# A decoder layer on one core: the value products of the first head pair placed before the next scores, and another order at the end of the merged stage

## The reference

```python
h = rmsnorm(x, attn_norm[l]) * (1.0 + scale_a) + shift_a
proj = h @ w_in[l]
y_mla = mla_mix(...)   # 8 heads, causal: softmax(qn kn + qp kp) @ v, then rmsnorm
y_gdn = gdn_mix(...)   # 4 heads, gated delta rule over chunks, then rmsnorm * silu(gate)
x = x + gate_a * (jnp.concatenate([y_mla, y_gdn], axis=-1) @ w_out[l])
h = rmsnorm(x, moe_norm[l]) * (1.0 + scale_m) + shift_m
x = x + gate_m * hierarchical_moe(h, ...)   # top group, top 2 of its 8 experts
return rmsnorm(x, final_norm)
```

## Time and profile before

| | us |
|---|---|
| median of 3 runs (2413.59 to 2421.41) | 2417.65 |
| the profiled execution, its own time | 2419.23 |
| its span, first to last instruction | 2417.5 |
| the merged stage in it | about 693 to 1476 |
| the output stage in it | 1476 to 1776 |

### The profile page before, as it was taken

How to read it: one execution, slowest core, us unless ns; L and a number is a source line. 1 busy time by engine, 2 the same in 40 slices (tenths; PEclk the granted TensorE clock), 3 DMA queues, 4 the chain that set the end, 5 groups by cost and what they waited for, 6 DMA issues and landing times. The chain is left out here.

```text
span 2417.5 us, 35480 instructions
## 1 busy us (share of the span) xinstructions
PE 2182.2 (90%) x11479; PEld 1243.3 (51%) x11480; DVE 987.8 (41%) x2202; ACT 872.1 (36%) x2123; POOL 631.6 (26%) x1108
## 2 busy tenths in 40 slices
PE   5999999999977998999999996999939999999990
PEld 2545555545444666666666673555534444444440
DVE  2334343433255575665566652234351222222223
ACT  2264363462655654555555561111111111111113
POOL 1000000000024542634542501233322222222224
PEclk9999999999988999999999998999969999999995
DMA  9212121120352344343343329333305788999777
GB/s 345 83 62 77 44 77 62 42 75 33 107 190 77 113 154 143 92 130 117 112 140 108 99 73 324 147 121 124 122 18 169 222 253 268 301 328 291 223 220 302
DMA packets 221896, 361.77 MB, mean 150 GB/s; under 512 B 45579, under 2 KB 143526, under 8 KB 218294
## 3 DMA queue, kind: packets, MB, share of 16 engines
q1 hardware_dynamic: 207926, 309.57, 37.6%
q0 software_dynamic: 13824, 50.34, 8.5%
HBM read 259.93 MB, written 99.93 MB: 149 GB/s over the span
## 5 line engine op out<-in xcount | busy, mean ns | idle before, releaser
L704 PE MATMUL pV<-keys_values_then_all,w_in_sb 128*128 128x512 f32 x768 | 341.3, 598 | 4.7 <-DMA w_in_sb<-in_w_in_dram 4.7
L2190 PE MATMUL hidden_ps<-w,keys_values_then_all 128*128 x752 | 331.5, 594 | 0.4 <-SPq L2062 0.4
L1252 ACT ACTIVATE probs<-scores,neg_max 128x512 f32<-128x512 f32 (+3 forms) x320 | 195.0, 621 | 227.6 <-DVE neg_max L1363 152.9
L704 PEld LDWEIGHTS pV<-keys_values_then_all,w_in_sb 128*128 128x128 f32 x768 | 145.1, 192 | 178.0 <-issue 177.3
L2190 PEld LDWEIGHTS hidden_ps<-w,keys_values_then_all 128*128 128x128 f32 x752 | 143.4, 191 | 180.6 <-issue 180.5
L1828 PE MATMUL out_ps<-keys_values_then_all 128*128 128x512 f32 x512 | 226.3, 601 | 2.5 <-ACT keys_values_then_all L1677 2.5
L2120 ACT ACTIVATE keys_values_then_all<-hidden_ps 128x256 f32<-128x256 f32 x47 | 18.0, 383 | 454.7 <-PE hidden_ps L2190 454.7
L2200 PE MATMUL expert_ps<-w_sb,keys_values_then_all 128*128 x368 | 169.8, 604 | 0.0
L1828 PEld LDWEIGHTS out_ps<-keys_values_then_all 128*128 128x128 f32 x512 | 97.2, 192 | 121.8 <-issue 116.2
L1169 POOL TENSOR_TENSOR keys_values_then_all<-keys_values_then_all 32x31 f32<-32x31 f32 (+15 forms) x248 | 120.5, 486 | 117.9 <-DMA keys_values_then_all<-a_d 98.7
L1508 PE MATMUL scores<-keys_values_then_all,queries 64*128 64x512 f32 (+3 forms) x640 | 148.0, 584 | 0.0
(11 more groups left out here) (371 smaller groups left out, 3196.6 us busy)
## 6 DMA issues: line engine op xcount, KB each, us to landing
w<-in_w_dram SPq DMA_DIRECT2D x64, 1024.0 KB, 10.4
w_sb<-in_w_dram SPq DMA_DIRECT2D x32, 1024.0 KB, 13.7
keys_values_then_all<-in_x_dram SPq DMA_DIRECT2D x32, 512.0 KB, 5.3
w_mod_rows<-in_w_mod_dram SPq DMA_DIRECT2D x16, 1024.0 KB, 4.9
keys_values_then_all<-in_w_mod_dram SPq DMA_DIRECT2D x4, 2048.0 KB, 15.0
qkv_d<-l_out SPq DMA_DIRECT2D x32, 256.0 KB, 2.3
keys_values_then_all<-y_d SPq DMA_DIRECT2D x16, 512.0 KB, 4.6
x_d<-keys_values_then_all SPq DMA_DIRECT2D x16, 512.0 KB, 2.9
```

The costliest lines, as they stand in the source:

```text
L704: last = pe.matmul(pV[n % 2][:], win[:, k, QKV0 + c * P:QKV0 + (c + 1) * P], hT[:, s % 2, k, :], start=(k == 0), stop=(k == ND - 1))
L1252: act.activation(prob[:, e, 0:w].rearrange("p t k -> p (t k)"), pS[e][:, 0:w * P], ACT.Exp, scale=-1.0, bias=nmin[:, i % 2, h, b:b + 1], a ...
L2190: last = pe.matmul(pH[par][:], xT[par][:, k], m.w13[:, ds(slot, 1), k].rearrange("p s n -> p (s n)"), start=(k == 0), stop=(k == ND - 1))
```

## The change

In `mix_order` the value products of a quad are two atoms instead of one. V(j, 0) comes behind T2 T3 and ahead of the first O and of S(j+1), V(j, 1) stays where both were; each costs half. The chain steps of the cost 0.325 n that stood between S(j+1) and V(j, 0) thereby come ahead of S(j+1). The steps held back (O2, G) go in behind V(j, 1), as before. In the last atoms BX(15) changes places with AS(14), and O2(15) comes behind the last O instead of ahead of it. SP loads the gate of chunk n+1 at TR(n) instead of at O2(n), with the same wait. In `output`, PE no longer waits at the start for the routing weights and for `pick`, but where it first uses them.

```diff
@@ -735,18 +735,19 @@
         if i > 1 and first and TILE[i - 1] < 4:
             atoms.append((0.0, [("AS", i - 2, 0)]))
         turns = [(0.13 * (TILE[i - 1] // 4 + 1), [("O", i - 1, hp)]) for hp in (2 * o, 2 * o + 1)] * (i > 0 and o < AH // 4)
+        atoms.append((0.325 * n, [("V", j, 0)]))
         atoms += turns[:1]
         if ahead:
             atoms.append((0.8 * ahead, [("S", j + 1)] + [("X", j + 1, e) for e in range(4)]))
         if i and last and TILE[i] >= 4:
             atoms.append((0.0, [("AS", i - 1, 0)]))
-        atoms.append((0.65 * n, [("V", j, 0), ("V", j, 1)]))
+        atoms.append((0.325 * n, [("V", j, 1)]))
         atoms += turns[1:]
         if i and o == AH // 4 - 1:
             atoms.append((0.0, [("A", i - 1, 0)]))
         if last:
             atoms.append((0.0, [("B", i, 0)]))
-    atoms.append((0.0, [("AS", NT - 2, 0), ("BX", NT - 1, 0), ("B2", NT - 1, 0)]))
+    atoms.append((0.0, [("BX", NT - 1, 0), ("AS", NT - 2, 0), ("B2", NT - 1, 0)]))
     for o in range(AH // 2):
         atoms.append((0.44, [("O", NT - 1, o)]))
     atoms.append((0.0, [("A", NT - 1, 0), ("AS", NT - 1, 0)]))
@@ -796,12 +797,12 @@
         while atoms and owed >= atoms[0][0]:
             owed -= atoms[0][0]
             order += atoms[0][1]
-            if atoms.pop(0)[1][0][0] == "V":
+            if atoms.pop(0)[1][0][::2] == ("V", 1):
                 order += held
                 held = []
-    order += held
-    for _, kinds in atoms:
+    for _, kinds in atoms[:-1]:
         order += kinds
+    order += held + atoms[-1][1]
     return quads, order
 
 
@@ -1089,6 +1090,9 @@
                     sp.dma_start(m.inv_d[n * (P - QK):(n + 1) * (P - QK), :], both_T).then_inc(inv_stored, 16)
                 elif kind == "L":
                     load_inverses(n)
+                elif kind == "TR" and n + 1 < NT:
+                    wait(yg_stored, 16 * n)
+                    load_gate(n + 1)
                 elif kind == "KS" and n + 2 < NT:
                     wait(ks_ready, n + 1)
                     load_kq(n + 2)
@@ -1101,9 +1105,6 @@
                         for r in range(8):
                             sp.dma_start(m.mod_d[0:1, r * 512:(r + 1) * 512], mod_sum[32 * (r % 4):32 * (r % 4) + 1, r // 4]).then_inc(mod_stored, 16)
                 elif kind == "O2":
-                    wait(yg_stored, 16 * n)
-                    if n + 1 < NT:
-                        load_gate(n + 1)
                     wait(yg_ready, n + 1)
                     sp.dma_start(m.y_d[n * P:(n + 1) * P, AH * DV:], gates[:, n % 2].rearrange("p h d -> p (h d)")).then_inc(yg_stored, 16)
                 elif kind == "V" and step[2] == 1 and n in last_j:
@@ -1809,8 +1810,6 @@
             start_counts(pe, sems[4::5])
             wait = waiter(pe)
             pe.wait_ge(m.wo_loaded, 16 * 2)
-            pe.wait_ge(m.wr_loaded, 16 * 6)
-            pe.wait_ge(pick_made, 3)
 
             def body(n, par, ty, mm, rt, lg):
                 if n in RANK_AT:
@@ -1847,6 +1846,8 @@
                     if n >= RANK_AT[0]:
                         pe.wait_ge(rank_read, sum(at <= n for at in RANK_AT))
                     pe.wait_ge(halves_copied, n - 1)
+                    if n == 2:
+                        pe.wait_ge(pick_made, 3)
                     wait(logit_read, n - 2)
                     pe.matmul(pL, halves_T[:], pick[:], start=True, stop=True).then_inc(logit_ready, 1)
                 if rt:
@@ -1854,6 +1855,8 @@
                     wait(h2T_dve, n)
                     if n > 1:
                         pe.wait_ge(halves_copied, n - 1)
+                    else:
+                        pe.wait_ge(m.wr_loaded, 16 * 6)
                     for k in range(ND):
                         at = 64 * (k % 2)
                         last = pe.matmul(pLT[at:at + NR, :], wr[:, k], h2T[:, k], start=(k < 2), stop=(k >= ND - 2))
```

## The result

| | before | after |
|---|---|---|
| median of the runs, us | 2416.38 (2413.59 to 2421.41) | 2440.93 (2435.03 to 2451.04) |
| profiled execution: time, span, us | 2419.23, 2417.5 | 2435.03, 2433.3 |
| TensorE busy, us | 2182.2 | 2202.0 |

The changed kernel is slower: ratio 1.01 with a 95 % interval of 1.0077 to 1.0123, +24.5 us between the medians. The forecast was 2434, slower. The two profiled executions differ by only 15.8 us, because that of after happens to be the fastest of its four and that of before lies 2.9 above its median. What follows compares the two profiles; the first experiment, whose profile lies on its median, supplies the rest.

What follows compares the result with a forecast made beforehand. The prediction saw TensorE, busy 2182.2 of 2417.5 us, waiting on a loop between scores through DVE and ACT. Terms +29.6 - 9 + 3 - 5.5 - 1.9 = +16.2 on 2419.2 gave 2435.4, stated as 2434; range 2396 to 2454.

Steps and rivals of the forecast that it cites:

- S wait: Merged stage: TensorE's waits ahead of the scores for copies of turned probabilities fall from 37.8 us to 2.7.
- V wait: Merged stage: V(j, 0) waits for the copies of heads 0 and 1, 53.8 us, 58 places over 0.1.
- The T wait: Merged stage: the transposes T wait 10.9 us more for their exponentials.
- No instruction is added: Merged stage: splitting the pair only moves 80 half value products of up to 0.95 us and adds no instruction.
- The other waits: Merged stage: TensorE's remaining waits, 28.5 us, partly shrink behind longer ones; from 0 to -28.5, taken as -9.
- The clock: Merged stage: more waits over 1.7 us, about 10 instead of 5, lower TensorE's clock; -6 to +15, taken as +3.
- The rival in which the clock gives everything back: Merged stage: waits cut too short to lower the clock bring 30 us back, 2401 us; chance 0.02.
- The last steps: Merged stage's end: BX(15) ahead of AS(14) and the earlier gate load end the stage sooner, -5.5 us.
- TensorE's start: Output stage: without the wait for POOL's `pick` TensorE starts at once, -1.9 us; later waits 0.
- the first (V waits for nothing): Merged stage: V(j, 0) fills the gap because ACT's copies come earlier; 2386 us, half of it 2400; chance 0.22.
- The second (waits only change their names): Merged stage: new waits at V and T replace chain waits one for one; 2411 us, or 2425; chance 0.22.
- The third (ACT's loop becomes the bound): Merged stage: with V(j, 0) inside ACT's loop other waits don't shrink; +37, 2455 us; chance 0.06.

Runs made afterwards that it cites:

- the first experiment: Kernel before with only the split: V(j, 0) its own atom ahead of the first O and S(j+1), end and loads as before; 2441.73 us, ratio 1.0119.
- third kernel: Changed kernel with V(j, 0) reading a constant tile, without its wait for copies; 2451.32 us, ratio 1.0156, later parts longer because other experts are chosen.
- ninth kernel: Kernel before with O placed between V(j, 0) and V(j, 1) in the 30 quads that have an O behind both; 2413.38 us, ratio 0.9988.
- second kernel: Changed kernel with the V pair together again as before; end order, gate load and output start stay changed; 2412.4 us, ratio 0.9998.
- seventh: Changed kernel with the V pair together again and the last tile's A and AS in another buffer; 2414.08 us, ratio 0.9988.
- fifth kernel: Changed kernel with head 1's copy moved from ACT to DVE, so each copies two turned heads; 2432.35 us, ratio 1.006.

## Why the prediction was right, and where its numbers were not

**Direction and place were right.** The S wait was to go and a V wait to come in its place: -37.6 and +43.8 measured, -35.1 (37.8 down to 2.7) and +53.8 in the sum. The third kernel shows the mechanism by taking the copies away, the first that the split alone does it.

**The V wait was mis-sized**, 53.8 for 43.8. I had placed V(j,0) by the planner's costs, but kept the ends of the copies where they were before; chain work that moved ahead of S may have left ACT freer between exponentials and copies. That this is the reason was not shown.

**The T wait** was put at +10.9. As a wait it came out at -2.4; but the T steps are 11.1 longer. Of the 224 T steps of full width, which take 0.44 us at the least, 25 took over 0.6 in before and 51 in after, and none more than 0.66, near the pace of the exponentials (0.67 each by the prediction's 1097.58 to 1100.25). I had written that L1516's wait would rise from 4.6 to 10 to 20, and it fell to 2.5. That T(j,0) to T(j,2), 6.6 us longer in all, follow the exponentials in step is argued from that pace; no run took it apart. The other 4.5 us are T(j,3)'s. At full width it takes 0.53 us ahead of V(j,0) also in most quads of the third kernel, where V hardly waits, so that a good part of it is the price of the place and not a wait for exponentials. That the whole came out at 11.1, next to the 10.9 of the sum, is in part luck.

**"No instruction is added" was the step that failed.** The moved products were costed at nothing, and cost 12.2 us; the ninth kernel shows it as a fixed price for each pair. The trace of before already had a sign of it: the same 16 products took 0.924 as V(j,0), which V(j,1) follows, and 0.974 as V(j,1), which something else follows. That missing term, 12.2, and the waits at S and V, which were over-sized by 12.5 (18.7 in the sum, 6.2 measured), nearly cancel. That 2434 came out near is luck to this extent.

**The other waits** shrank by 8.6, for 9 forecast. That was a third of a bound from 0 to -28.5, so in part luck.

**The clock** was put at +3, for about ten waits over 1.7 us at S and V instead of five. There are four instead of five, and the stage's clock is 0.97 for 0.96: no cost. The 9.3 us that the profile of after stood less at the 1.2 GHz level go with its 4.2 us less of S steps, but the first experiment, with the same split, has neither (51.2 us at the low level as before), and among executions of before's own order it was 41.0 to 54.6. So that gain is the execution's and not shown to be the change's. The rival in which the clock gives everything back leaned on what the Trainium skill says of the clock ("TensorE: Matmul & The Clock Gate", Part 1: it is halved after idling, and half of the time spent so is lost). The traces show the lower level behind waits of TensorE; how much of the time spent there is lost, no run here takes apart. The rival itself isn't borne out, for 41.9 us at the low level were left.

**The last steps** were put at -5.5 and gave +0.3. BX did come ahead of AS and the wait for the gate did go, both as foretold; the next in line was one I had not named, the buffer `ya`, whose store is queued behind loads of which I knew that they land late. I had let AS(15)'s store queue behind them and forgotten AS(14)'s. In the split's absence the same edits give -1.5 (second kernel), and -3.9 with the buffer (seventh). Against the first experiment, which has the split and the end of before and took 22.7 us from V to SP, they give -1.0.

**TensorE's start** was put at -1.9 and gave -1.5; the output stage then took 1.2 more, because the load of `y` of the third tile, behind the expert loads, is now waited for 4.8 us instead of 3.5. Single waits scatter: 2.3 to 4.0 us in the four profiles that have the start of before, 3.3 to 4.8 in the eight with the earlier start and all 12 loads ahead. I had looked at what is ready, not at what is still being loaded.

**The sum** was +16.2 against the profiled execution; between the profiled executions it is +15.8, between the medians +24.5. The two profiles flatter it: that of after was the fastest of its four. The measured median lies 6.9 us above the 2434 that I stated, well inside the range. Of the rivals, the first (V waits for nothing) falls with the 42.6 us of L1530. The second (waits only change their names) is right for the waits, which sum to less than before, and wrong for the time, since the steps grew. The third (ACT's loop becomes the bound) falls with the fifth kernel: taking a copy from ACT gave 8.6, no more than in the kernel before.

## What to carry to other kernels

When work is moved from the shadow of one wait to a place ahead of the next, list what that work itself needs: here the two copies, so that one wait was only exchanged for another. Then cost the *seams* too: here each pair of value products taken apart cost 0.15 us in its own steps, 12 us in all, and a transpose directly ahead of them cost 0.09 more. Compare the distances between the starts of steps, not only the waits. Where a wait is removed, look at every other thing that ended in its shadow, stores and single buffers above all, and where loads of megabytes are issued ahead, ask which small transfers stand behind them.

## What the runs showed of the hardware

- A step of 16 value products (weights 128 x 64) takes 0.924 us up to the next step where other work is ahead and value products follow, 0.974 where value products are ahead and other work follows, and 1.025 where other work is on both sides. For steps of 4 products it is 0.269, 0.320 and 0.370: the same differences. The records' own durations hardly show it (281 and 284 ns in the mean); the distance between the steps' starts does.
- A step of four transposes takes 0.44 us at the least ahead of TR, DS, K or O, and 0.53 at the least ahead of V, WU, Y or M.
- One order of the merged stage stood for 41.0 to 54.6 us at the 1.2 GHz level from one execution to another (before, second and seventh kernel), and its S steps sum to 217.3 to 222.0 us with it.
- A store of 256 KB that lands 2.0 us after its issue in the median took 8.6 us behind loads that had been issued 13 to 19 us ahead of it. In the output stage a load of `y` behind 12 expert loads cost TensorE 2.3 to 4.8 us. Moving six of these loads by a tile or two took the wait away, and 5.6 us of the stage with it.
